# Decay levels of two chunked scans: the score matmuls stream only the second-half queries, and one strided predicated copy a level takes them over

## The reference

```
b = cumsum(log_f)                       # inside a chunk, per key channel
decay  = where(causal, exp(b_t - b_s), 0)
scores = sum_k q[t,k] * decay[t,s,k] * k[s,k]
o      = (q * exp(b)) @ S + scores @ v
S_new  = exp(b_last) * S + (k * exp(b_last - b)).T @ v
```

## Time and profile before

| | us |
|---|---|
| median of 3 runs | 3677.16 (3673.34 to 3688.01) |
| the profiled execution | 3682.05 |
| its span, first to last instruction | 3680.2 |
| mean granted TensorE clock | 0.933 of 2.4 GHz |

### The profile page before, as it was taken

How to read it: one execution, slowest core, us unless ns; L and a number is a source line. 1 busy time by engine, 2 the same in 40 slices (tenths; PEclk the granted TensorE clock), 3 DMA queues, 4 the chain that set the end, 5 groups by cost and what they waited for, 6 DMA issues and landing times. The chain is left out here.

```text
span 3680.2 us, 52818 instructions
## 1 busy us (share of the span) xinstructions
PE 3290.3 (89%) x21119; PEld 3020.7 (82%) x21119; DVE 1304.4 (35%) x2147; ACT 994.0 (27%) x1598; POOL 793.3 (22%) x420
## 2 busy tenths in 40 slices
PE   7997798999566789999999999967677899999998
PEld 6996455777455689999999989956557899999998
DVE  4111344555468243222222231127552422222223
ACT  3002133444344232222222220024431322222222
POOL 2211001343233121222122121114221222122211
PEclk9998898999667899999999999978788999999999
DMA  3322003776121311111111022232213111111111
GB/s 102 91 88 84 28 12 135 281 277 240 62 73 36 101 35 47 46 44 41 46 46 46 26 85 87 89 117 104 79 61 107 40 47 40 46 46 45 41 46 71
DMA packets 230478, 288.56 MB, mean 78 GB/s; under 512 B 11792, under 2 KB 193488, under 8 KB 230368
## 3 DMA queue, kind: packets, MB, share of 16 engines
q1 hardware_dynamic: 211648, 203.10, 17.2%
q0 software_dynamic: 18720, 83.92, 6.5%
HBM read 237.50 MB, written 49.48 MB: 78 GB/s over the span
## 5 line engine op out<-in xcount | busy, mean ns | idle before, releaser
L657 POOL TENSOR_TENSOR mlp_w_lo<-mlp_raw,mlp_w_hi 128x1024 fp32r<-128x1024 f32 x126 | 302.9, 2404 | 1239.1 <-ACT mlp_w_hi L618 1239.1
L96 PE MATMUL mlp_bank<-mlp_x_hi,mlp_w_hi 128*128 128x352 f32 (+1 forms) x1536 | 504.1, 328 | 12.9 <-DVE mlp_w_lo L344 12.0
L96 PE MATMUL mlp_bank<-mlp_a_hi,mlp_w_hi 128*128 128x352 f32 (+1 forms) x1536 | 502.5, 327 | 0.9 <-DVE mlp_a_lo L684 0.9
L98 PE MATMUL mlp_bank<-mlp_x_hi,mlp_w_lo 128*128 128x352 f32 (+1 forms) x1536 | 503.0, 327 | 0.0
L97 PE MATMUL mlp_bank<-mlp_x_lo,mlp_w_hi 128*128 128x352 f32 (+1 forms) x1536 | 502.7, 327 | 0.0
L98 PE MATMUL mlp_bank<-mlp_a_hi,mlp_w_lo 128*128 128x352 f32 (+1 forms) x1536 | 502.6, 327 | 0.0
L97 PE MATMUL mlp_bank<-mlp_a_lo,mlp_w_hi 128*128 128x352 f32 (+1 forms) x1536 | 502.0, 327 | 0.0
L700 DVE TENSOR_TENSOR xT<-xT,mlp_bank 128x352 f32<-128x352 f32 (+1 forms) x384 | 202.7, 532 | 527.2 <-PE mlp_bank L98 527.2
L618 ACT ACTIVATE mlp_w_hi<-mlp_raw 128x1024 fp32r<-128x1024 f32 x126 | 132.6, 1053 | 645.5 <-PE mlp_bank L98 645.5
L96 PEld LDWEIGHTS mlp_bank<-mlp_x_hi,mlp_w_hi 128*128 128x128 f32 x1536 | 289.8, 189 | 14.0 <-DVE mlp_w_lo L344 12.6
L97 PEld LDWEIGHTS mlp_bank<-mlp_x_lo,mlp_w_hi 128*128 128x128 f32 x1536 | 290.8, 189 | 0.0
(11 more groups left out here) (429 smaller groups left out, 5705.0 us busy)
## 6 DMA issues: line engine op xcount, KB each, us to landing
mlp_raw<-in_w_down SPq DMA_DIRECT2D x64, 512.0 KB, 3.3
mlp_raw<-in_w_up SPq DMA_DIRECT2D x62, 512.0 KB, 4.0
projections<-odd_zout SPq DMA_DIRECT2D x24, 544.0 KB, 3.1
odd_raw<-in_w_in_odd SPq DMA_DIRECT2D x23, 512.0 KB, 4.4
projections<-even_zout SPq DMA_DIRECT2D x21, 544.0 KB, 3.2
even_raw<-in_w_in_even SPq DMA_DIRECT2D x20, 512.0 KB, 4.5
evenout_mixed<-mixed SPq DMA_DIRECT2D x8, 544.0 KB, 6.3
gla_v<-projections SPq DMA_DIRECT2D x4, 1088.0 KB
```

The source lines that it names most:

```text
L96: pe.matmul(out, w_hi, x_hi, start=first, stop=False)
L98: return pe.matmul(out, w_lo, x_hi, start=False, stop=last)
L657: pool.tensor_tensor(w_lo[:, t % 2, :], raw[:, t % 2, :], r32(w_hi[:, t % 2, :]), ALU.subtract).then_inc(lo_done, 1)
```

## The change

For levels 1 to 7 only the queries in second halves can pair with a key, which is half the columns of every chunk. The changed kernel gives PE only these as moving columns: 64 for a chunk instead of 128, picked with a stride from `x`, and 32 instead of 64 for the samples. The stationary operand stays the whole 128 x 128 block of `x`. The results of 8 chunks are 8 x 64 values a partition, which is one PSUM bank, so a level takes one bank (`S[2]` or `S[3]` in turn) where it took two. One predicated copy takes the whole bank, with a strided mask and a strided destination in `a`. Level 0 is as before. Waits and semaphores are the same.

```diff
+        def later_half(li):
+            return S[2 + li % 2][:].rearrange("p c t -> p (c t)").rearrange("p (c t) -> p c t", t=P // 2)
...
-                    for g in range(2):
-                        last = dve.copy_predicated(a[:, 4 * g:4 * g + 4, :],
-                                                   levels[:, li:li + 1, :].broadcast_to([P, 4, P]), S[2 * (li % 2) + g][:])
-                    if li < LS:
-                        last = dve.copy_predicated(a[0:NS, C, 0:NS], levels[0:NS, li, 0:NS],
-                                                   (SS, U)[li % 2][0:NS, 0:NS])
+                    if li == 0:
+                        for g in range(2):
+                            dve.copy_predicated(a[:, 4 * g:4 * g + 4, :],
+                                                levels[:, 0:1, :].broadcast_to([P, 4, P]), S[g][:])
+                        last = dve.copy_predicated(a[0:NS, C, 0:NS], levels[0:NS, 0, 0:NS], SS[0:NS, 0:NS])
+                    else:
+                        m = LEVELS[li - 1]
+                        n = P // (2 * m)
+                        seen = half(levels[:, li, :], m, True)
+                        last = dve.copy_predicated(
+                            a[:, 0:C, :].rearrange("p c (n m) -> p c n m", m=2 * m)[:, :, :, m:2 * m],
+                            seen.unsqueeze(1).broadcast_to([P, C, n, m]),
+                            later_half(li).rearrange("p c (n m) -> p c n m", m=m))
+                    if 0 < li < LS:
+                        last = dve.copy_predicated(half(a[0:NS, C, 0:NS], m, True), half(levels[0:NS, li, 0:NS], m, True),
+                                                   (SS, U)[li % 2][0:NS, 0:NS // 2].rearrange("p (n m) -> p n m", m=m))
...
-                        last = pe.matmul(S[2 * (li % 2) + c // 4][:, c % 4, :], first[:, t], second[:, t],
-                                         start=True, stop=True)
+                        if li == 0:
+                            last = pe.matmul(S[c // 4][:, c % 4, :], first[:, t], second[:, t], start=True, stop=True)
+                        else:
+                            last = pe.matmul(later_half(li)[:, c, :], first[:, t], half(second[:, t], LEVELS[li - 1], True),
+                                             start=True, stop=True)
                     if li < LS:
-                        last = pe.matmul((SS, U)[li % 2][0:NS, 0:NS], first[:, SEQ:T], second[:, SEQ:T],
-                                         start=True, stop=True)
+                        own_t, cols = second[:, SEQ:T], NS
+                        if li:
+                            own_t, cols = half(own_t, LEVELS[li - 1], True), NS // 2
+                        last = pe.matmul((SS, U)[li % 2][0:NS, 0:cols], first[:, SEQ:T], own_t, start=True, stop=True)
```

## The result

The changed kernel takes 3710.12 us in the median of 8 runs (3696.27 to 3716.28), against 3676.72 in the median of 8 runs of the kernel before on the same chip: ratio 1.0086, 95% interval 1.0068 to 1.0104, 33 us or 0.9% slower. 3708 was predicted.

What follows compares the result with a forecast made beforehand. The scan's levels were taken as bound by the ring POOL, DVE, POOL (3.20 us a period). With PE at a low clock, HGRN2 adds 18.7 us and GLA 12.6, 31 in sum, moving the median from 3677 to 3708; range 3665 to 3724.

Steps and rivals of the forecast that it cites:

- main case: Scan levels: narrow matmuls drop the clock to 1.2 GHz through the levels; 3708 us (3692 to 3724), chance 0.72.
- Level 2 to the first state update, 24.4 us.: One head's span at the low clock, from levels, transposes and handoffs; in HGRN2 head 0 it was 19.0 before.
- PE becomes the bound.: Levels at the low clock: PE still works when its next `x` is ready, and DVE waits for PE in each `keep`.
- HGRN2, 18.7 us.: Time added over four HGRN2 heads: 5.0 each for heads 0 and 2, 3.1 for head 1, 5.6 for head 3.
- The gates' part in it, 0.4: HGRN2 heads 0 and 2: DVE's later gates meet less of POOL's L1701, which gives back some 0.4 us.
- GLA, 12.6 us.: Time added over four GLA heads: 2.3 each for even heads, DVE's idle for ACT absorbing some, and 4.0 each for odd.
- Two batches of state updates at 2.08: Tail of odd GLA heads: two batches at 2.08 us instead of 1.10, with about 1 us of outputs, 3 more.
- The term that decided, the clock.: Scan levels: 64-column matmuls let the clock fall soon after level 1, to 1.2 GHz until the tail's wide matmuls.
- The copy: Predicated copy, one instead of two: 0.67 us, saving 0.65 a level, worth 1.3 a head in `keep(5)` and `keep(7)`.
- The clock stays: Main rival, scan levels: the clock stays high and the shorter copies save about 12 us, 3665; chance 0.16.
- It falls but comes back: Rival: nine transposes raise the clock for levels 4 to 7; about 12 us more, 3689; chance 0.08.
- DVE's queue: Rival: DVE sets the levels' period, so each shorter copy saves 0.65 us; 36 us less, 3641; chance 0.04.

Runs made afterwards that it cites:

- experiments 1: Changed kernel with levels 1 to 7 back at 128 matmul columns, keeping the single short strided copy; 3674.16 us against 3677.28 before, ratio 0.9986.
- 2: Changed kernel plus one unread 512-column matmul a level: from level 2 on, ratio 1.0091 to the kernel before; from level 1 on, 1.0042.
- experiment 6: Changed kernel with only some levels 64 columns wide, the others 128: levels 1 to 3 narrow, 0.9997 of the kernel before; levels 4 to 7 narrow, 1.0028.
- 4: Changed kernel with 32 instead of 64 columns in levels 2 to 7, half of those scores stale; ratio 1.0086 to the kernel before.
- the wide kernel: Changed kernel with 128-column matmuls again in levels 1 to 7 and the single short strided copy kept; 3674.16 us, ratio 0.9986 to the kernel before.
- experiment 5: Changed kernel with every predicated copy of levels 1 to 7 made once more into a scratch tile; 3723.8 us, ratio 1.0122 to the kernel before.
- e11: Changed kernel plus one unread 512-column matmul in each of levels 1 to 7; ratio 1.0042 to the kernel before.
- e2: Changed kernel plus one unread 512-column matmul in each of levels 2 to 7; ratio 1.0091 to the kernel before.
- e1: Same run as the wide kernel: 128-column matmuls again in levels 1 to 7, short copy kept; ratio 0.9986 to the kernel before.
- e10: Kernel before with only the first batch of state updates moved up behind level 5's matmuls; ratio 0.9989 to the kernel before.

## Why the prediction was right

The main case had the mechanism and the size. That 3708 lay 2 us from 3710.12 is in part luck: the terms below miss by up to 2 us a head, up and down, and the heads add up to 28.1 us in the traces where 31 were forecast and 33.4 measured in the medians. By its own terms:

- **"Level 2 to the first state update, 24.4 us."** HGRN2 head 0: 1010.10 - 985.67 = 24.43. Levels 2 and 3 took 7.25 with PE's last two short waits (7.9 less 1.0 was forecast), the transposes 2.13 (2.2), levels 4 to 7 13.91 (14.0), the handoff 1.14 (1.3). In HGRN2 head 1, GLA head 0 and GLA head 2 it was 24.44 each, in HGRN2 heads 2 and 3 and GLA head 3 24.92, 25.13 and 25.21, where the fall came earlier, and in GLA head 1 26.11.
- **PE becomes the bound.** DVE's L1943 now waits for PE's L2059 37.8 us in HGRN2 (16 times), where the like wait before was 6.2 us (6 times).
- **HGRN2, 18.7 us.** Measured 17.6: +5.0 and +5.4 for the even heads (5.0 each), +2.8 (3.1) and +4.4 (5.6) for the odd ones. In head 3 two errors met: the levels grew by 3.3 and not 2.6, the tail by 1.2 and not 3. The gates' part in it, 0.4, came out in the tails of heads 0 and 2.
- **GLA, 12.6 us.** Measured 10.5: +0.7 and +2.5 for the even heads (2.3 each), +3.6 and +3.7 for the odd ones (4.0 each). In head 0 the levels grew by the 5.4 expected, but the tail gave back 4.7 and not 3.1. DVE's wait for ACT is gone, as was said: L1877 follows its `keep(7)` at once, where L1873 had idled 3.10 us.

```profile
2523.92 0.72 DVE L1943 COPY_PREDICATED gla_a<-gla_levels,gla_S 128x512 f32<-128x512 int32 x1 [2.69 <-PE gla_S L2059]
2524.54 1.27 DVE L1877 SCALAR_TENSOR_TENSOR gla_logf<-gla_f_raw,gla_soft 128x1088 f32<-128x1088 f32 x1
```

- **"Two batches of state updates at 2.08"** in the odd GLA heads: the trace has them, at 2.05 and 1.82. With the outputs the tails grew by 1.6 and 1.9 us, not 3; the levels of head 1 grew by 2.0, not 1.0: its `scale(5)` still stood behind `v_own` (from 2581.71 to 2584.96, 3.25 us instead of 1.3), so that the slow levels did not hide all of it.

```profile
2593.32 2.05 PE L2098 MATMUL gla_U<-gla_v_tok,gla_k_tok 128*128 128x256 f32 x4 [1.15 <-DVE gla_a L1943]
...
2596.40 1.82 PE L2098 MATMUL gla_U<-gla_v_tok,gla_k_tok 128*128 128x256 f32 x4 [0.18 <-DVE gla_state L1970]
```

- **The term that decided, the clock.** It was argued from rows of other stages; experiments 1, 2, 6 and 4 showed it: with wide matmuls the clock holds, the same narrow matmuls with wide ones beside them hold it too, wide levels bring it back, and fewer columns change nothing more once it is low. The Trainium skill's page "TensorE: Matmul & The Clock Gate" ties the fall to idle gaps ("Why this matters for your kernels"). The trace does not agree for the changed kernel, and the measurement decides: PE is busy for 13.91 of 13.91 us at 0.50. In the kernel before, with gaps of about 1 us, it is busy for 10.49 of 13.40 us at 1.00.
- **The copy** was taken at 0.67 between 0.65 and 1.33. From level 3 on it takes 0.70 to 0.73; in levels 1 and 2, the upper bound, 1.29 and 1.30. It stands behind POOL's difference there (988.92 to 990.89), so it cost nothing.

The rivals. The clock stays: false, 0.55 to 0.61 in the mean of levels 1 to 7 of a head. It falls but comes back: false for this kernel, as nine transposes do not bring it back, but true as soon as four wide levels follow (experiment 6). DVE's queue: false; the wide kernel has the shorter copies in levels 3 to 7, which would be 5 x 8 x 0.6 = 24 us by that rival, and gained 5, and doubling every copy (experiment 5) cost 14 and not 40.

## What to carry to other kernels

Halving the columns of a matmul whose time does not depend on them saves next to nothing (0.05 us a level here), and can cost the clock for that stage and the work behind it; look first whether the granted clock is held by the columns that you are about to remove. A loop in which PE idles can hold the high clock, and one in which it never idles can lose it, so idle time alone does not say. When a stage may lose its clock, ask what stands around it: narrow levels cost less with wide ones behind them (4 us) or ahead of them (15 us) than both together (37 us). And look at the tails: a stretch whose clock can fall or hold makes single traces differ by 6 us in one head.

## What the runs showed of the hardware

- A recorded matmul instruction with 128 x 128 fp32 weights of its own (two for one matmul) takes 0.125 to 0.128 us at the high clock (2.00 us for sixteen of 64 columns, 2.05 of 128) and 0.217 us at the low one (13.86 us for sixty-four of 32 columns, 13.91 of 64).
- One matmul of 512 columns a level held the clock through levels 2 to 5 of all eight heads (e11), and where it had fallen before, it was back at 1.00 after two filled levels and the transposes (1060.44 in e2); with the narrow matmuls alone it never came back within the levels, in eight heads.
- Wide matmuls do not always bring it back soon: behind the samples' 8-column matmuls of GLA head 3 in e1, matmuls of 352 to 512 columns ran at 0.50 with PE busy for 9.00 of 9.00 us.
- A predicated copy of 128 x 512 fp32 values from PSUM takes 1.29 us when its destination is in runs of 1 or 2 values, 0.69 to 0.73 when it is dense or in runs of 4, 16 or 64. A strided mask changes neither time (1.29 and 1.29, 0.72 and 0.72).
- The kernel before took 3677 us on one chip and 3800 us on others. It was not traced there, but the kernel of e10 was: its HGRN2 scan starts 125 us later (1107.80 against 982.49), and from the start of the GLA scan to the end it takes 1197 us against 1200. From 600 to 900 us the DMA engines are busy for 0.75 to 0.80 of the time in the trace of the kernel before and for 0.52 to 0.59 in that of e10. At 434 us the two still agree (L961), and sample attention ends 125 us apart (L1330 at 948.44 and 1073.8).
